# Scores a pair ahead, sampled keys by halves and the key tail's order, in the attention of a hybrid decoder step

## The chip, the core and the metric

The kernel runs on one core of a Trainium2 chip. It is one program that computes a whole inference step. The metric is the device time of one execution in microseconds (us). PE is TensorE, DVE is VectorE, ACT is ScalarE, POOL is GpSimd and SP is SyncE. Every one of them runs its own list of instructions in order, and they wait for each other only by semaphores.

## The reference, cut to what matters

Two layers, each on 256 prompt positions and on 8 sampled sequences of 4 new tokens with 2048 past positions each. Every layer has one input projection, an S5 state-space group, a sparse attention group with 8 query heads and 2 key/value heads, an output projection and a SwiGLU FFN. The change touches attention only. For each query head it is

```
def dense_gqa(q, k, v, dist, valid):
    s = einsum('...tkgd,...skd->...kgts', q, k) * HEAD_DIM ** -0.5
    s = s - alibi_slopes()[:, :, None, None] * dist[..., None, None, :, :]
    p = masked_softmax(s, valid[..., None, None, :, :])
    return einsum('...kgts,...skd->...tkgd', p, v), p
```

done three times (compressed blocks, the 16 of 33 key blocks of 64 with the highest summed compressed probability, and a sliding window of 512) and added with sigmoid gates. For the prompt every branch sees at most 256 keys. For the samples the selected branch has 2048 cached keys per sequence, which are read from a paged cache: 16 pages of 128 positions each, keys and values apart, 128 KB a page and kind.

## The kernel before

All activations lie in SBUF with the features on the partitions; 288 columns are the 256 prompt tokens and the 32 sampled ones. A layer is a hardware loop over the same code: projection with the state-space scan beside it, the compression of 256 cache pages by convolution, then **the attention middle** (at 683 to 797 us and 2556 to 2669 us in the profile), **the value stage** in which the cached values are weighted (to 882 and 2753 us), then output projection and FFN, which are plain streams of weights through PE.

In the attention middle two things run interleaved, by an order that is written out by hand in each engine's program.

- *Sampled keys.* The keys of the 8 sequences come in half groups: 2 halves (`hf`) of 4 groups (`g4`), each in two sets `e` (even and odd sequences). SP and POOL each load one half of every set, four pages, in `key_pages` (L286 to L297): four register loads of page numbers, then a wait for `kring_free`, then four DMAs. A set's buffer is free when `keys` (L820, on PE, matmuls at L827) has multiplied the set two before it. Two window sets of `keys` go first, then 16 cache sets, four for each pair of prompt heads. The scores of the 128 sampled rows land in banks 2 and 3 of PSUM (`PS[1]`, one bank for each key head, 512 columns). DVE adds the position bias and takes them to SBUF (`biased`, L1572), for a full group at once, and allows the next group with `kgroup_evac`.
- *Prompt heads.* The 8 heads go in pairs, `HEADS[0]` and `HEADS[1]`, each with two banks for scores (`h.s1`, `h.s0`; banks 0, 1 and 4, 5) and its own buffers. For a head: POOL copies its queries (`h.q`, L522) and gives `q_copied`; PE computes `scores` (L850, L856); DVE `prompt_bias` (L1640) adds the bias and takes maxima; ACT takes exponentials (L1200); DVE `prompt_scale` (L1656) normalizes (last operation at L1669); PE turns the probabilities (`turn_p`, L862, into banks 6 and 7); ACT takes them back (L1204 to L1206, `pt_evac`); PE weights the values (`weigh`, L873) into `h.s1`, the head's own score bank; DVE `prompt_out` (L1671) copies them out and gives `po_evac`, which the next `scores` of this buffer waits for.

The order on PE for a pair (`pair`, L884) is: scores of both heads, two `keys` sets, turn head a, one `keys` set, weigh a, turn b, one `keys` set, weigh b. On DVE: bias a, bias b, scale a, scale b, out a, the group of sampled keys, out b, then for the sampled keys the block mask (added at L1696) and the maxima (L1698). On POOL (L518 to L526), for pair i: the two query copies of pair i, then its four sets. So the copies for pair i+1 stand behind the last set of pair i.

After the fourth pair DVE takes the last maxima (`sw_max`), ACT takes the exponentials of the sampled scores (`SS`, 2080 wide, then `SW`, 544 wide, for both key heads, L1213), DVE normalizes (`sw_ready`), PE turns them in 12 steps through 6 banks (L922) and ACT takes each to `PTS` (L1222, L1226). Then the value stage: `values` (L311 to L322) loads 16 pages of each sequence from three queues ("full" by SP, "more" by POOL, "rest" by ACT, five or six pages each, again with register loads first), into two buffers in turn. The first needs all key sets done (`kring_free` 22); the second lies over `SS` and needs all 12 turns done (`st_done` 12).

Of the kernel before, what the change touches and what calls it, by code (L numbers as in the profile page):

```python
# [23 lines left out]
P = 128  # L24
# [84 lines left out]
def build(nc, T):  # L109
# [174 lines left out]
    with nc.Fori(0, L) as lay:  # L284
        with nc.Block() as block:
# [302 lines left out]
            QKG = [C_QN] * 4 + [C_KS, C_KW]  # L588

            @block.tensor  # L590
            def _(pe):
# [228 lines left out]
                def keys(hf, e, count, more=None):  # L820

                    pe.wait_ge(S[f"kset{e}_full"], count)
                    if more is not None:
                        pe.wait_ge(S[f"kset{e}_more"], more)
                    for k in range(NKV):
                        for j in range(4):
                            mm = pe.matmul(PS[1][32 * j:32 * j + 32, k, 256 * hf:256 * hf + 256].rearrange("p (g s) -> p g s", g=2),  # L827
                                           QPD[:, k, 2 * j + e, :], KR[4 * e + j][:, :, k, :], start=e == 0, stop=e == 1,
                                           tile_position=(0, 32 * j))
                    mm.then_inc(S["kring_free"], 1)  # L830

                pe.wait_ge(S["kgroup_evac"], 1)
# [51 lines left out]
                def pair(n, g4, k, peeled=False):  # L884
                    a, b_ = HEADS
# [17 lines left out]
                pair(0, 0, 0, peeled=True)  # L903
                pair(2, 1, 0)
                with pe.Fori(0, 2) as i:
                    pair(2 * i + GQA, i + 2, 1)
# [3 lines left out]
                pe.wait_ge(S["sw_ready"], 2)  # L910
                blocks = [(SS, x, P) for x in range(16)] + [(SS, 16, SMP)] + [(SW, x, P) for x in range(4)] \
                    + [(SW, 4, SMP)] + [(SCM, 0, NCMP)]
                for n in range(12):
                    if n >= 6:
                        pe.wait_ge(S["st_evac"], n - 5)
                    for m, (src, x, w) in enumerate(blocks[2 * n:2 * n + 2]):
                        if src is SW and x == 0:
                            pe.wait_ge(S["sw_ready"], 3)
# [1000 lines left out]
```

## Time and profile before

| | |
|---|---|
| median of 3 runs (lowest, highest) | 3755.5 us (3750.58, 3756.93) |
| the profiled execution, its own time | 3758.73 us |
| its span in the profile | 3757.2 us |
| PE busy | 3313.9 us, 88% |
| DVE / ACT / POOL busy | 48% / 32% / 21% |
| granted PE clock, mean | 0.924 |
| SP page issues of keys, POOL page issues of keys | 128 and 128, 128 KB each |
| median time from issue to landing of these | 2.4 us (SP), 2.9 us (POOL) |

The busy shares are means over stages with different limits. The change touches some 115 us of each layer, in which PE is not busy all the time, so what it is worth has to be read from the timelines of this stretch. Register loads and waits are not counted as busy; on POOL they show as idle time before a DMA ("issue").

### The profile page before, as it was taken

The numbers are of one execution on the slowest core, as the hardware profiler recorded it, in microseconds if no ns is written. First come the engines' busy times: TensorE is split into PE (matmuls) and PEld (weight loads), VectorE is DVE, ScalarE is ACT, GpSimd is POOL, SyncE is SP. The second block draws the span as 40 slices with busy tenths as digits, with TensorE's granted clock in tenths as the row PEclk, the third lists the DMA queues.
The fourth block names the chain that finished last, engine by engine and source line by source line (L and its number), as shares of the span: only waits on it lengthen the run. The fifth ranks groups of instructions, "written<-read, shape, count | busy, mean of one in ns | idle before, by whom it ended". The sixth has DMA issues, their size and how long they took to land. (4 is left out here: it accounts for less than half of the span.)

```text
span 3757.2 us, 62333 instructions
## 1 busy us (share of the span) xinstructions
PE 3313.9 (88%) x21882; PEld 2936.5 (78%) x21882; DVE 1820.4 (48%) x2671; ACT 1206.8 (32%) x1445; POOL 793.9 (21%) x1515
## 2 busy tenths in 40 slices
PE   6799699767899999999977995997678999999998
PEld 4566477546799999999955664775477999999998
DVE  4666555542433333444456665556433333334444
ACT  2011255232333333333320112552323333333333
POOL 1666523222100000000026664222221000000000
PEclk8788799878999999999977887998789999999999
DMA  4224535565344444444331244355653444444443
GB/s 156 77 98 167 190 108 186 169 210 194 134 151 162 158 172 161 156 164 171 113 121 68 93 191 163 126 177 172 217 193 117 157 170 165 156 172 163 157 159 134
DMA packets 142918, 579.44 MB, mean 154 GB/s; under 512 B 20817, under 2 KB 92658, under 8 KB 116530
## 3 DMA queue, kind: packets, MB, share of 16 engines
q1 hardware_dynamic: 106706, 491.88, 36.1%
q0 software_dynamic: 23968, 71.07, 5.8%
q10 hardware_dynamic: 12096, 14.69, 1.2%
q8 instruction: 72, 1.18, 0.1%
q14 instruction: 76, 0.62, 0.0%
HBM read 570.02 MB, written 24.18 MB: 158 GB/s over the span
## 5 line engine op out<-in xcount | busy, mean ns | idle before, releaser
L988 PE MATMUL banks<-normed_hi,weights_hi 128*128 128x288 f32 x4736 | 1408.1, 297 | 55.3 <-POOL normed_lo L534 34.1
L988 PE MATMUL banks<-normed_lo,weights_hi 128*128 128x288 f32 x4736 | 1399.8, 296 | 0.0
L988 PE MATMUL banks<-normed_hi,weights_lo 128*128 128x288 f32 x4736 | 1395.0, 295 | 0.0
L1327 DVE TENSOR_TENSOR weights_lo<-weight_slots,weights_hi 128x2048 fp32r<-128x2048 f32 x296 | 680.7, 2300 | 1103.5 <-ACTq L1252 1103.5
L988 PEld LDWEIGHTS banks<-normed_hi,weights_hi 128*128 128x128 f32 x4736 | 890.3, 188 | 57.9 <-issue 55.0
L1249 ACT ACTIVATE weights_hi<-weight_slots 128x2048 fp32r<-128x2048 f32 x296 | 567.0, 1916 | 1142.6 <-PE banks L988 1134.8
L988 PEld LDWEIGHTS banks<-normed_hi,weights_lo 128*128 128x128 f32 x4736 | 894.7, 189 | 0.0
L988 PEld LDWEIGHTS banks<-normed_lo,weights_hi 128*128 128x128 f32 x4736 | 892.1, 188 | 0.6
L344 DVE TENSOR_TENSOR arena<-arena 128x192 f32<-128x192 f32 (+5 forms) x800 | 425.4, 553 | 44.8
L344 POOL TENSOR_TENSOR arena<-arena 128x64 f32<-128x64 f32 (+5 forms) x800 | 408.0, 520 | 86.2 <-issue 0.7
L605 PE MATMUL banks<-normed,weight_slots 128*128 128x288 f32 x1664 | 421.9, 417 | 0.0
L605 PEld LDWEIGHTS banks<-normed,weight_slots 128*128 128x128 f32 x1664 | 324.9, 196 | 97.3 <-issue 6.0
L794 PE MATMUL banks<-conv_high,conv_weights 128*128 128x508 f32 x1024 | 335.4, 409 | 27.1 <-DVE conv_low_a L1327 18.8
L794 PEld LDWEIGHTS banks<-conv_high,conv_weights 128*128 128x128 f32 x1024 | 194.8, 192 | 82.2 <-issue 15.4
L1175 ACT ACTIVATE conv_high<-arena 128x512 fp32r<-128x512 f32 x256 | 158.0, 628 | 172.7 <-PE banks L794 172.5
L308 POOL DMA_DIRECT2D arena<-in_cache_cmp x256 | 137.4, 537 | 317.0 <-issue 303.5
L483 POOL DMA_DIRECT2D params<-in_params x2 | 1.2, 616 | 865.2 <-issue 865.2
L1037 ACT ACTIVATE projected<-banks 128x576 f32 (+1 forms) x28 | 18.2, 651 | 419.6 <-PE banks L605 401.5
L657 PE MATMUL banks<-arena 128*32 128x288 f32 x256 | 32.7, 685 | 129.4 <-issue 129.4
L657 PEld LDWEIGHTS banks<-arena 128*32 128x32 f32 x256 | 13.4, 161 | 144.6 <-issue 144.6
L1327 DVE TENSOR_TENSOR conv_low_a<-arena,conv_high 128x512 fp32r<-128x512 f32 x128 | 86.6, 691 | 79.1 <-ACT conv_high L1175 77.7
L1327 DVE TENSOR_TENSOR conv_low_b<-arena,conv_high 128x512 fp32r<-128x512 f32 x128 | 87.7, 691 | 69.9 <-ACT conv_high L1175 68.8
(271 smaller groups left out, 2683.0 us busy)
## 6 DMA issues: line engine op xcount, KB each, us to landing
weight_slots<-in_w_gu SPq DMA_DIRECT2D x88, 2048.0 KB, 7.6
weight_slots<-in_w_down SPq DMA_DIRECT2D x44, 2048.0 KB, 7.7
weight_slots<-in_w_in SPq DMA_DIRECT2D x28, 2048.0 KB, 7.7
arena<-in_cache_cmp SPq DMA_DIRECT2D x256, 128.0 KB, 3.3
arena<-in_cache_cmp POOLq DMA_DIRECT2D x256, 128.0 KB, 3.4
weight_slots<-in_w_out SPq DMA_DIRECT2D x16, 2048.0 KB, 7.9
arena<-in_cache_slc_k SPq DMA_DIRECT2D x128, 128.0 KB, 2.4
arena<-in_cache_slc_k POOLq DMA_DIRECT2D x128, 128.0 KB, 2.9
```

The costliest lines, as they stand in the source:

```text
L308: eng.dma_start(AR[:, o:o + 256], T["cache_cmp"][bass.ds((lay * 160 + page) * 2 + k, 1)] .rearrange("a p x -> p (a x)")).then_inc(S[f"raw{ ...
L344: return eng.tensor_tensor(out, a, b, op)
L483: pool.dma_start(PR[:, :], row("params", lay)).then_inc(S["params_in"], 16)
L605: mm = pe.matmul(banks_[:, m, 0:TOK], WR[:, s, c, 128 * m:128 * m + 128], rhs(first + c), start=start and c == 0, stop=stop and c == k - 1)
L657: mm = pe.matmul(PS[2][o:o + 32, j // 4, 0:TOK], CBS[:, j, r, :], HS[:, j, r, :], start=r == 0, stop=r == 1, tile_position=(0, o))
L794: mm = pe.matmul(acc, w, x, start=i == hf == 0 and x is hi and w is wh, stop=i == 15 and hf == 1 and x is lo)
L988: mm = pe.matmul(out, wt[:, hf, col], x[:, rhs + c, :], start=begin and c == 0 and i == 0, stop=hf == 1 and c == k - 1 and i == 2, skip_gr ...
L1037: act.activation(dst, src, ACT.Copy).then_inc(S[sem], by)
L1175: act.activation(HRG[:, n % 4, :].rearrange("p (g x) -> p g x", x=16), RAW[u % 2][:, :, i, :], ACT.Copy)\
L1249: w = act.activation(WH[:, hf, :], WR[:, s, 8 * hf:8 * hf + 8, :].rearrange("p a b -> p (a b)"), ACT.Copy)
L1327: return dve.tensor_tensor(out, a, b, op)
```

## The change

It rewrites the order of the attention middle; what is computed stays the same.

- PE: `scores` of pair i+1 move from behind both `weigh` of pair i to before `turn_p` of pair i. Scores no longer wait for `po_evac` but for `ps_max`. Both `weigh` now stand at the end of the pair, write to bank 3 and wait for `po_evac` once a pair. All eight `keys` halves write 256 columns for each key head into bank 2, and the first set of each half waits for `kgroup_evac` of the half before it, the window halves too.
- DVE: sampled keys go out by halves (256 columns, `keys_out`); the bias of the next pair stands between the two halves; both heads' outputs go out in one copy behind the second half.
- ACT: the exponentials of pair i+1 stand behind the `pt_evac` of pair i.
- The pair loops are written out, with constant addresses.
- Tail: `SW` before `SS` in exponentials, normalization and turns (`TURNS`), and ACT's five value pages of the first sequence (`values(act, 0, 0, "rest")`) move from before the exponentials to behind them.
- The programs of POOL and SP are not changed.

```diff
+            TURNS = [9, 10, 11] + list(range(9))
@@ PE
-                def keys(hf, e, count, more=None):
+                def keys(n, e, count, more=None):
...
+                    if e == 0:
+                        pe.wait_ge(S["kgroup_evac"], n + 1)
...
-                            mm = pe.matmul(PS[1][32 * j:32 * j + 32, k, 256 * hf:256 * hf + 256].rearrange("p (g s) -> p g s", g=2),
+                            mm = pe.matmul(bank(2)[32 * j:32 * j + 32, 256 * k:256 * k + 256].rearrange("p (g s) -> p g s", g=2),
...
-                pe.wait_ge(S["kgroup_evac"], 1)
...
                 def scores(n, h, k):
                     pe.wait_ge(S["q_copied"], n + 1)
-                    pe.wait_ge(S["po_evac"], n + 1)
+                    if n >= 2:
+                        pe.wait_ge(S["ps_max"], n - 1)
...
                 def weigh(n, h, k):
                     pe.wait_ge(S["pt_evac"], n + 2)
-                    o = h.s1
+                    if n % 2 == 0:
+                        pe.wait_ge(S["po_evac"], n + 2)
+                    o = bank(3)[:, 256 * (n % 2):256 * (n % 2) + 256]
...
+                scores(0, a, 0)
+                scores(1, b_, 0)
+                for i in range(4):
+                    n = 2 * i
                     def part(hf, e):
-                        keys(hf, e, g4 * 128 + 64 * hf + 192, g4 * 128 + 64 * hf + 64)
-                    scores(n, a, k)
-                    scores(n + 1, b_, k)
-                    pe.wait_ge(S["kgroup_evac"], g4 + 2)
+                        keys(2 + n + hf, e, 128 * i + 64 * hf + 192, 128 * i + 64 * hf + 64)
                     part(0, 0)
                     part(0, 1)
-                    if peeled:
+                    if i == 0:
                         mask()
+                    if i < 3:
+                        scores(n + 2, a, (n + 2) // GQA)
+                        scores(n + 3, b_, (n + 3) // GQA)
                     turn_p(n, a)
                     part(1, 0)
-                    weigh(n, a, k)
+                    part(1, 1)
                     turn_p(n + 1, b_)
-                    part(1, 1)
-                    weigh(n + 1, b_, k)
+                    weigh(n, a, n // GQA)
+                    weigh(n + 1, b_, n // GQA)
...
+                for i, n in enumerate(TURNS):
+                    if i >= 6:
+                        pe.wait_ge(S["st_evac"], i - 5)
+                    if i in (0, 3):
+                        pe.wait_ge(S["sw_ready"], 2 if i == 0 else 3)
@@ ACT
+                for j, h in enumerate(HEADS):
+                    prompt_exp(j, h)
+                for i in range(NQ // 2):
                     for j, h in enumerate(HEADS):
                         act.wait_ge(S["pt_done"], 2 * i + j + 3)
...
-                values(act, 0, 0, "rest")
+                    if i < 3:
+                        for j, h in enumerate(HEADS):
+                            prompt_exp(2 * i + 2 + j, h)
 
                 act.wait_ge(S["sw_max"], 1)
-                for i, v in enumerate((SS, SW)):
+                for i, v in ((1, SW), (0, SS)):
...
+                values(act, 0, 0, "rest")
@@ DVE
-                dve.wait_ge(S["kring_free"], 6)
-                for k in range(NKV):
-                    biased(SW[:, k, 0:WIN], dw[:, 0:WIN], k, PS[1][:, k, :])
-                dve.drain().then_inc(S["kgroup_evac"], 1)
+                for hf in range(2):
+                    dve.wait_ge(S["kring_free"], 2 * hf + 4)
+                    for k in range(NKV):
+                        biased(SW[:, k, 256 * hf:256 * hf + 256], dw[:, 256 * hf:256 * hf + 256], k, bank(2)[:, 256 * k:256 * k + 256])
+                    dve.drain().then_inc(S["kgroup_evac"], 1)
...
+                for i in range(NQ // 2):
                     n = 2 * i
                     prompt_scale(n, a)
                     prompt_scale(n + 1, b_)
-                    prompt_out(n, a)
...
+                    keys_out(i, 0)
+                    if i < 3:
+                        prompt_bias(n + 2, a)
+                        prompt_bias(n + 3, b_)
+                    keys_out(i, 1)
+                    prompt_out(n)
```

## Rows read from the trace of the kernel before

**Rows 1.** windows: length, PE, PEld, DVE, ACT, POOL busy, PE clock, DMA share, GB/s

```profile
725.13:746.04 20.91, 15.62 (x125) 10.35 (x124) 13.50 (x38) 7.11 (x30) 9.32 (x18) 0.92 0.67 199
...
814.00:882.00 68.00, 43.24 (x776) 32.39 (x776) 11.39 (x26) 8.80 (x19) 16.66 (x32) 0.80 0.87 294
```

**Rows 2.** timeline of POOL, layer 0: start, us, operation, count [idle before, releaser]

```profile
697.34 2.31 POOL L294 DMA_DIRECT2D arena<-in_cache_slc_k  x4 [12.93 <-PE banks L827]
702.30 2.32 POOL L294 DMA_DIRECT2D arena<-in_cache_slc_k  x4 [2.66 <-issue]
...
714.64 0.74 POOL L522 COPY squares<-projected 128x256 f32 x2
719.24 0.54 POOL L294 DMA_DIRECT2D arena<-in_cache_slc_k  x1 [3.85 <-PE banks L827]
721.81 1.73 POOL L294 DMA_DIRECT2D arena<-in_cache_slc_k  x3 [2.04 <-issue]
...
778.82 2.32 POOL L294 DMA_DIRECT2D arena<-in_cache_slc_k  x4 [2.66 <-issue]
```

**Rows 3.** timeline of POOL, layer 1, same columns

```profile
2569.73 2.31 POOL L294 DMA_DIRECT2D arena<-in_cache_slc_k  x4 [12.65 <-PE banks L827]
...
2632.35 1.26 POOL L522 COPY squares<-projected 128x256 f32 x2
...
2652.58 2.32 POOL L294 DMA_DIRECT2D arena<-in_cache_slc_k  x4 [2.64 <-issue]
```

**Rows 4.** timeline of TensorE, layer 0, same columns

```profile
694.70 1.93 PE L827 MATMUL banks<-arena 128*32 128x256 f32 x16 [4.34 <-DMA arena<-in_win_k]
...
714.71 0.47 PE L866 MATMUL banks<-consts,weight_slots 128*128 128x128 f32 x1 [3.78 <-DVEq L1669]
...
716.61 1.94 PE L827 MATMUL banks<-arena 128*32 128x256 f32 x16
...
720.68 0.33 PE L866 MATMUL banks<-consts,weight_slots 128*128 128x128 f32 x1
...
721.70 1.07 PE L827 MATMUL banks<-arena 128*32 128x256 f32 x16
723.00 0.70 PE L877 MATMUL banks<-weight_slots,v_rows 128*128 128x256 f32 x2 [0.22 <-ACTq L1207]
...
725.13 0.71 PE L856 MATMUL banks<-projected,squares 128*128 128x128 f32 x4
...
728.74 1.07 PE L827 MATMUL banks<-arena 128*32 128x256 f32 x16
...
788.84 1.07 PE L827 MATMUL banks<-arena 128*32 128x256 f32 x16 [2.25 <-DMA arena<-in_cache_slc_k]
789.84 0.78 PE L877 MATMUL banks<-weight_slots,v_rows 128*128 128x256 f32 x2
```

**Rows 5.** timeline of TensorE, layer 1, same columns

```profile
2572.55 1.22 PE L856 MATMUL banks<-projected,squares 128*128 128x128 f32 x4
...
2577.59 1.07 PE L827 MATMUL banks<-arena 128*32 128x256 f32 x16
```

**Rows 6.** timeline of VectorE, layer 0, same columns

```profile
691.83 2.49 DVE L1327 TENSOR_TENSOR arena<-arena 64x1089 f32<-64x1089 f32 x2
...
793.98 1.28 DVE L1327 TENSOR_TENSOR arena<-arena  x2
```

**Rows 7.** timeline of ScalarE, layer 0, same columns

```profile
791.15 2.42 ACTq L320 DMA_DIRECT2D arena<-in_cache_slc_v  x5
797.30 2.03 ACT L1213 ACTIVATE arena<-arena,smalls 128x2080 f32<-128x2080 f32 x1 [9.56 <-DVE smalls L1708]
...
805.01 0.60 ACT L1222 ACTIVATE arena<-banks 128x512 f32<-128x512 f32 x1 [1.48 <-PE banks L922]
...
813.53 0.39 ACT L1222 ACTIVATE arena<-banks 127x256 f32<-127x256 f32 x1
816.90 2.77 ACTq L320 DMA_DIRECT2D arena<-in_cache_slc_v  x5
```

More of the change, by code:

```diff
@@ L1194, in _, with prompt_exp @@
                 act.drain().then_inc(S["c_exp"], 1)
-                with act.Fori(0, NQ // 2) as i:
-                    for j, h in enumerate(HEADS):
-                        act.wait_ge(S["ps_max"], 2 * i + j + 1)
-                        for c, v in enumerate([h.p1[:, 0], h.p1[:, 1], h.p0[:, 0], h.p0[:, 1], h.pc[:, 0], h.pc[:, 1]]):
-                            act.activation(v, v, ACT.Exp, bias=h.m[:, c:c + 1], accum_out=h.d[:, c:c + 1])
-                        act.drain().then_inc(S["p_exp"], 1)
+                def prompt_exp(n, h):
+                    act.wait_ge(S["ps_max"], n + 1)
+                    for c, v in enumerate([h.p1[:, 0], h.p1[:, 1], h.p0[:, 0], h.p0[:, 1], h.pc[:, 0], h.pc[:, 1]]):
+                        act.activation(v, v, ACT.Exp, bias=h.m[:, c:c + 1], accum_out=h.d[:, c:c + 1])
+                    act.drain().then_inc(S["p_exp"], 1)
+                for j, h in enumerate(HEADS):
+                    prompt_exp(j, h)
+                for i in range(NQ // 2):
                     for j, h in enumerate(HEADS):
@@ L1215, in _ @@
                         act.drain().then_inc(S["sw_exp"], 1)
+                values(act, 0, 0, "rest")
                 widths = [P] * 16 + [SMP] + [P] * 4 + [SMP] + [NCMP]
-                for n in range(12):
-                    act.wait_ge(S["st_done"], n + 1)
+                for i, n in enumerate(TURNS):
+                    act.wait_ge(S["st_done"], i + 1)
                     w = widths[2 * n:2 * n + 2]
-                    src = bank([0, 1, 4, 5, 6, 7][n % 6])
+                    src = bank([0, 1, 4, 5, 6, 7][i % 6])
                     if len(set(w)) == 1:
@@ new lines, in keys_out @@
+                def keys_out(i, hf):
+                    c = slice(512 * i + 256 * hf, 512 * i + 256 * hf + 256)
+                    dve.wait_ge(S["kring_free"], 4 * i + 2 * hf + 8)
+                    for k in range(NKV):
+                        biased(SS[:, k, c], ds_[:, c], k, bank(2)[:, 256 * k:256 * k + 256])
+                    dve.drain().then_inc(S["kgroup_evac"], 1)
+                a, b_ = HEADS
+                prompt_bias(0, a)
+                prompt_bias(1, b_)
+                dve.wait_ge(S["mask_done"], 1)
@@ L1691, in pair @@
-                    dve.drain().then_inc(S["kgroup_evac"], 1)
-                    prompt_out(n + 1, b_)
-                    for k in range(NKV):
-                        v = SS[:, k, bass.ds(i * 512, 512)].rearrange("p (j s) -> p j s", s=SEL)
-                        tt(v, v, MB[:, k, bass.ds(i * 8, 8)].unsqueeze(2).to_broadcast([P, 8, SEL]), ALU.add)
+                    keys_out(i, 0)
+                    if i < 3:
+                        prompt_bias(n + 2, a)
+                        prompt_bias(n + 3, b_)
@@ L1700, in _ @@
-                dve.wait_ge(S["tables_back"], 16)
-                pair(0, peeled=True)
-                with dve.Fori(1, 4) as i:
-                    pair(i)
+                        dve.tensor_reduce(mxs[:, k, i:i + 1], SS[:, k, 512 * i:512 * i + 512], AXX, ALU.max)
                 dve.drain()
```

47 lines of the change are left out of this document (15 added, 32 removed).

## The prediction, written before the changed kernel ran

> **What bounds the kernel now.** I read the page first (PE 88% busy), then the windows of the attention middle, then the timeline of each engine there. In a window of one pair of heads PE works 15.6 of 20.9 us and the DMA share is 0.67, against 0.87 in the value stage [rows 1]: neither the array nor the transfers bound this stage. Two loops run through it side by side. The first is the chain of a pair, scores, bias, exponential, scale, turn, weigh, out: PE sits idle 3.78 us before the first turn and waits there for DVE [rows 4]. The change is aimed at this one. The second is POOL's list. A set of four pages takes 2.32 us of issues and 2.66 us of register loads before them, and the two query copies of a pair 0.74 us [rows 2]. Four sets and the copies make 4 x (2.32 + 2.66) + 0.74 = 20.7 us, and the pair's window has 20.9. So POOL already sets the pace, and shortening the first loop alone could take at most what POOL waits: its sets run from 697.34 to 781.14 (83.8 us) in layer 0 and from 2569.73 to 2654.90 (85.2 us) in layer 1 [rows 2, 3], against 16 x 2.32 + 15 x 2.66 + 3 x 0.74 = 79.2 us.
>
> **The sum is made against the profiled execution,** 3758.7 us, 3.2 above the median of 3755.5 us; the difference is put on the median at the end.
>
> **Scores ahead: a new loop through POOL.** Scores of heads n+2 and n+3 now stand on PE before the turn of head n and before the third set of keys. They need the query copies, and POOL makes these behind the pair's fourth set. That fourth set needs the second `keys` of the same pair, so POOL can't have it early. What is queued behind the waiting scores: both turns, two `keys` sets, both weighs. Who waits for that: POOL's and SP's first set of the next pair, which needs the third `keys`. So a round can't be shorter than this chain:
>
> - four sets with three groups of register loads: 4 x 2.32 + 3 x 2.66 = 17.3 us [rows 2]; the fourth group of loads is hidden in the wait;
> - the first query copy and its signal: half of 0.74 us and 0.1, 0.5 us [rows 2];
> - scores of two heads: 3.61 us at the upper clock level (725.13 to 728.74) [rows 4], 5.04 us where they began at the lower level (2572.55 to 2577.59) [rows 5]. PE will have waited for the copy by then, as it had in the 3.78 us before 714.71, where a turn then took 1.90 us instead of 1.02 (714.71 to 716.61, 720.68 to 721.70) [rows 4]. I take 5.0;
> - the turn, 1.02 us, and `keys`, 1.07 us, with the level back up (1.90 and 1.94 at the lower one) [rows 4];
> - from the end of `keys` to POOL's first issue: 696.63 to 697.34, 0.7 us [rows 2, 4].
>
> Sum 25.6 us a round. Bounds: 17.3 + 0.5 + 3.6 + 1.0 + 1.1 + 0.3 = 23.8 us, if the array keeps the upper level and the signal is short, and 17.3 + 0.9 + 6.7 + 1.9 + 1.9 + 0.8 = 29.5 us with all of it at the lower level (the scores' 3.61 us stretched as the turn is, 1.90 to 1.02). There are three such rounds in a layer, and one of them keeps the 2.04 us stall inside POOL's first set of the second pair [rows 2]. The last pair has no scores behind it, and its four sets take their 17.3 us. All sets then take 3 x 25.6 + 2.0 + 17.3 = 96.1 us: 12.3 us more than now in layer 0, 10.9 us in layer 1. The bounds give 90.7 and 107.8 us, so 5.5 to 24.0.
>
> The other effects of this part cost nothing while POOL is that late. The `ps_max` wait, the halves' `kgroup_evac` waits and the bias between the halves all lie in the 8 us in which POOL issues its last set. The written-out loops save a few issue gaps there.
>
> **The window halves.** PE's first `keys` of the second half ran at 694.70 [rows 4]. It now needs DVE's first half to be out, and DVE is in the comparisons until 694.32 [rows 6]; two additions of 256 columns (an estimate of 0.4 us each: 2.49 us for 2 x 1089 columns is 0.3 for 256, and something fixed) and a signal give 695.3. POOL's first set starts 0.6 us later; bounds 0 and 1.
>
> **The last sets' tail.** The last page set arrives as late behind its issue as now (781.14 to 788.84 [rows 2, 4]). Now `keys`, one weigh and one copy follow, and DVE begins the mask at 793.98, 5.1 us after 788.84 [rows 4, 6]. After the change `keys`, the turn of head 7, two weighs and a double copy stand between, as DVE takes the outputs before the mask. PE will have stood idle for some 8 us, so at the lower level: 1.9 + 1.9, then a weigh of 2.9 (2.1 us at the upper level from 723.00 to 725.13, 3.6 where the level fell from 789.84 on [rows 4]), a second of 2.1, the copy 0.7 (ACT's of 512 columns takes 0.60 [rows 7]): 9.6 us with signals. That is 4.5 us more; bounds 2 and 6.
>
> **The ScalarE handover.** ACT's five pages of the first sequence went out at 791.15, while ACT waited for the maxima [rows 7]: their price was nothing. They now stand behind the four exponentials and before the 12 copies of turned scores. A call of `values` on ACT costs its register loads too: after the last copy (813.92) the next call's issues began at 816.90 and ended at 819.67, 5.8 us [rows 7]. From the start of the exponentials at 797.30 they end 6.2 us later (805.01 less the 1.48 idle), the call takes 5.8, and the 12 copies 8.2 (805.01 to 813.92, less the short waits for PE): 20.2 us against 16.6. The windows' turns going first gain nothing, because ACT is in `SS`'s exponentials and the call by then. So 3.6 us later at the end and some 2.5 to 3 at the twelfth turn, which starts the second buffer's load. I take 3.2; bounds 0 (value stage absorbs it) and 3.7. What follows is a double-buffered stream of loads at a DMA share of 0.87 [rows 1], which makes nothing up.
>
> **Sum.** Layer 0: 12.3 + 0.6 + 4.5 + 3.2 = 20.6. Layer 1: 10.9 + 0.6 + 4.5 + 3.2 = 19.2. Together +39.8 us: 3798.5 against the profiled run, 3795 against the median.
>
> **Two rules weighed.** The query copies are on the path now. Their usual 0.74 us became 1.26 us at 2632.35 [rows 3]. The Trainium skill ("SBUF — State Buffer", Who interferes with whom) says that a DVE instruction with two SBUF inputs blocks a GpSimd one that reads SBUF. By it the copies stay short, since DVE will be idle and waiting for these very scores; by the stretched row each round gains 0.3 to 0.5 us, 3 us in all.
>
> The same skill ("TensorE: Matmul & The Clock Gate", HAM oscillation — how this bites in real kernels) says that an array that waits on data in every round restarts at its lower clock in every round. The turn's 1.90 us after a wait agrees. Without the rule the scores would cost 3.6 us instead of 5.0, 8 us less in all, and the result would be 3787.
>
> **Rivals.**
> *A, faster:* the first loop decides and POOL's copies come in time. For it speaks PE's idle 3.78 us before a turn. Against it, the copies stand behind the fourth set, and a pair already fills POOL. It decides if PE reaches the scores after the copies, which needs a round of PE's own work above 25 us where it has 15.6. POOL's waits of 4.6 and 6.0 us would go, 1.2 come back at the window halves: some 9 us less, 3746.
> *B, no change:* POOL's later sets only fill slack before the value stage. The sets' end and the mask are linked in one chain (788.84 to 793.98), so there is no slack. 3755.
> *C, slower by half:* rounds at 23.8 us and the handover absorbed: 2 x (6.2 + 0.6 + 2) = 18 us, 3773. For it: DVE and SP are not slowed.
> *D, slower still:* all of the loop at the lower level, 29.5 us: 2 x (23.3 + 0.6 + 6 + 3.7) = 67 us, 3822. For it: PE will idle in each round. Against it: the level was back 4 us after a wait, at 720.68 [rows 4].
>
> **How the numbers follow.** Mine 0.68, C 0.15, D 0.09, A 0.04, B 0.04. The predicted time is 3795. The range leaves out A, B and the far half of C and D: 3774 to 3811. A measurement of this kernel tells 0.2% (7.5 us) from no change: faster 0.04, within it 0.04, slower 0.92.
>
> **What would show it.** POOL's first set of pair i+1 should start 25 to 26 us after that of pair i, and its idle time before it be released by PE's L827. PE should be idle some 4 to 8 us before each later `scores`, released by POOL, and hardly before a turn. The mask should begin 9 to 10 us after the last `keys` starts, and five ACT issues should lie between the last exponential and the first copy of turned scores. I am wrong if POOL's rounds stay at 21 us, or if the value stage begins late but ends at its old distance from the last key set.

## The result, and the profile after

| | before | after |
|---|---|---|
| median of 4 runs beside each other (lowest, highest) | 3756.22 us (3750.58, 3757.8) | 3805.68 us (3802.0, 3811.0) |
| profiled execution, its span | 3757.2 us | 3802.3 us |
| granted PE clock, mean | 0.924 | 0.915 |

The changed kernel is slower: ratio 1.0131 (95% interval 1.0118 to 1.0143), 49.5 us on the medians and 45.1 us between the two profiled spans. The prediction said 3795 us and 39.8 us.

First the windows of the changed kernel, one round of POOL and the value stage, in the columns of [rows 1]:

```profile
755.03:781.42 26.39, 16.95 (x128) 11.97 (x124) 13.45 (x40) 7.11 (x30) 9.32 (x19) 0.74 0.50 160
836.00:904.00 68.00, 43.06 (x737) 32.23 (x739) 11.00 (x25) 12.19 (x26) 18.77 (x35) 0.77 0.84 280
```

The 26.39 us are POOL's third round, from its first set to that of the next pair; it is 5.5 us longer than the 20.91 of before, while DVE, ACT and POOL are busy for the same time. PE is busy 1.3 us more at a lower granted clock (0.74 for 0.92), and the transfers' share fell from 0.67 to 0.50. So the time is waiting, and not work.

The timeline of POOL shows where, in layer 0 (columns as in [rows 2]):

```profile
701.56 2.31 POOL L294 DMA_DIRECT2D arena<-in_cache_slc_k  x4 [14.05 <-PE banks L830]
...
718.86 1.20 POOL L522 COPY squares<-projected 128x256 f32 x2
727.43 0.54 POOL L294 DMA_DIRECT2D arena<-in_cache_slc_k  x1 [7.37 <-PE banks L830]
730.01 1.73 POOL L294 DMA_DIRECT2D arena<-in_cache_slc_k  x3 [2.04 <-issue]
...
746.72 0.74 POOL L522 COPY squares<-projected 128x256 f32 x2
755.03 2.32 POOL L294 DMA_DIRECT2D arena<-in_cache_slc_k  x4 [7.57 <-PE banks L830]
...
772.27 0.74 POOL L522 COPY squares<-projected 128x256 f32 x2
781.42 2.32 POOL L294 DMA_DIRECT2D arena<-in_cache_slc_k  x4 [8.40 <-PE banks L830]
...
796.37 2.32 POOL L294 DMA_DIRECT2D arena<-in_cache_slc_k  x4 [2.67 <-issue]
```

After each pair's copies POOL waits for PE's `keys` (now L830) 7.4 to 8.4 us, of which some 2.7 are its own register loads. The rounds are 25.9, 27.6 and 26.4 us, and all sets take 97.1 us (701.56 to 798.69) where they took 83.8. And PE, in the same stretch (columns as in [rows 4]), waits for those copies:

```profile
719.31 1.22 PE L859 MATMUL banks<-projected,squares 128*128 128x128 f32 x4 [5.09 <-POOL squares L522]
...
724.66 0.31 PE L869 MATMUL banks<-consts,weight_slots 128*128 128x128 f32 x1
...
725.66 1.93 PE L830 MATMUL banks<-arena 128*32 128x256 f32 x32
...
747.17 1.22 PE L859 MATMUL banks<-projected,squares 128*128 128x128 f32 x4 [5.97 <-POOL squares L522]
...
772.73 1.22 PE L859 MATMUL banks<-projected,squares 128*128 128x128 f32 x4 [5.72 <-POOL squares L522]
...
778.65 0.31 PE L869 MATMUL banks<-consts,weight_slots 128*128 128x128 f32 x1
```

Scores from their first matmul to the turn behind them took 5.35 us (719.31 to 724.66) and 5.92 us (772.73 to 778.65), against 3.61 us at the full clock in [rows 4]. The windows of the round between them, cut where the level changes, show why:

```profile
747.17:750.50 3.33, 3.33 (x12) 2.97 (x13) 0.00 (x0) 0.00 (x0) 0.29 (x1) 0.52 0.16 53
750.50:752.26 1.76, 1.76 (x15) 1.66 (x14) 0.00 (x0) 0.00 (x0) 0.00 (x0) 1.00 0.00 0
```

PE had been idle for 5.97 us; its clock was granted at 0.52 (nearly all at the level of 1.2 GHz) for the first 3.3 us of scores, and at 1.00 (2.4 GHz) behind that. In the rounds before and after it the first 3.5 us of scores had 0.50.

The end of the middle, first PE, then DVE, then ACT, in layer 0:

```profile
807.74 1.94 PE L830 MATMUL banks<-arena 128*32 128x256 f32 x16 [10.43 <-DMA arena<-in_cache_slc_k]
...
815.14 0.69 PE L886 MATMUL banks<-weight_slots,ssm_out 15*128 15x256 f32 x2
```

```profile
697.87 0.87 DVE L1581 SCALAR_TENSOR_TENSOR arena<-consts,banks 128x256 f32<-128x256 f32 x2 [0.44 <-issue]
...
815.94 0.69 DVE L1683 COPY normed<-banks 128x512 f32<-128x512 f32 x1 [5.33 <-PE banks L886]
816.55 1.28 DVE L1336 TENSOR_TENSOR arena<-arena 128x512 f32<-128x512 f32 x2
```

```profile
819.78 0.75 ACT L1221 ACTIVATE arena<-arena,smalls 128x544 f32<-128x544 f32 x1 [7.05 <-DVE smalls L1719]
...
829.27 2.44 ACTq L320 DMA_DIRECT2D arena<-in_cache_slc_v  x5
831.75 0.60 ACT L1231 ACTIVATE arena<-banks 128x512 f32<-128x512 f32 x1 [5.75 <-PE banks L925]
```

The mask starts 8.8 us behind the last `keys` (807.74 to 816.55; before, 788.84 to 793.98, 5.1 us). ACT's first copy of turned scores starts 12.0 us behind its first exponential (819.78 to 831.75; before, 797.30 to 805.01, 7.7 us), with register loads and the five issues in between.

Between anchors that both kernels have (the load of the tie table ahead of the stretch, POOL's first and last set, the last `keys`, the mask, the first exponential, the first matmul of the output projection) the two profiles give, in us, layer 0 / layer 1:

| stretch | before | after | more | forecast |
|---|---|---|---|---|
| tie table to first set | 14.2 / 13.9 | 15.3 / 15.5 | 1.1 / 1.5 | 0.6 |
| first to last set | 83.8 / 85.2 | 97.1 / 97.4 | 13.3 / 12.3 | 12.3 / 10.9 |
| last issue to last `keys` | 7.7 / 7.6 | 9.05 / 8.6 | 1.35 / 1.0 | 0 |
| last `keys` to mask | 5.1 / 3.7 | 8.8 / 8.6 | 3.7 / 4.9 | 4.5 |
| mask to first exponential | 3.3 / 3.3 | 3.2 / 3.2 | -0.1 | 0 |
| first exponential to output projection | 98.2 / 97.2 | 100.1 / 99.9 | 1.9 / 2.7 | 3.2 |
| together | 212.3 / 210.9 | 233.7 / 233.2 | 21.3 / 22.3 | 20.6 / 19.2 |

That is 43.6 of the 45.1 us between the profiled spans.

### The profile page after: what moved, and what is told of

It reads as the page before. It is cut to its first block, busy times and chain, and to the rows that moved or that the text cites. A ratio compares the mean times of both kernels' runs of the same rounds, so it can differ in the third digit from the quotient of the medians.

```text
span 3802.3 us, 62159 instructions
## 1 busy us (share of the span) xinstructions
PE 3323.5 (87%) x21882; PEld 2947.9 (78%) x21882; DVE 1819.2 (48%) x2683; ACT 1206.8 (32%) x1445; POOL 795.0 (21%) x1515
## 4 chain that ended last, share of the span: by engine, by line
PE 36%; DVE 5%; issue 3%; DVEq 1%; ACT 1%; DMA 1%; POOLq 1%; ACTq 1%; SPq 1%; POOL 0%; PEld 0%; PEldq 0%
PE banks L991 25%; PE banks L795 4%; DVE arena L344 3%; PE banks L606 3%; PE banks L645 1%; DVEq L358 1%; POOLq L289 1%; PE banks L658 0%; PE banks L859 0%; ACTq L315 0%; ACTq L320 0%; DMA arena<-in_cache_slc_v 0%; DVE arena L1336 0%; DVEq L383 0%; PE banks L598 0%
## 5 line engine op out<-in xcount | busy, mean ns | idle before, releaser
L606 PEld LDWEIGHTS banks<-normed,weight_slots 128*128 128x128 f32 x1664 | 325.2, 196 | 97.4 <-issue 6.0
L795 PEld LDWEIGHTS banks<-conv_high,conv_weights 128*128 128x128 f32 x1024 | 194.4, 192 | 82.2 <-issue 15.3
```

The source lines that it names most:

```text
L606: mm = pe.matmul(banks_[:, m, 0:TOK], WR[:, s, c, 128 * m:128 * m + 128], rhs(first + c), start=start and c == 0, stop=stop and c == k - 1)
L795: mm = pe.matmul(acc, w, x, start=i == hf == 0 and x is hi and w is wh, stop=i == 15 and hf == 1 and x is lo)
```

## The experiments

Each was timed beside the kernel before on the same chip; the ratio is to that kernel, with its 95% interval. The kernel before itself read 3756.1 to 3757.4 us in these batches. Differences to the changed kernel are taken from its 3805.7 us, which stands on a batch of its own with the kernel before at 3756.2 us. Each kernel has one profile, so a row of a single profile can be off by what varies from kernel to kernel; where that matters it is said.

### The copies alone

In the changed kernel only POOL's program is edited: the query copies of pair i+1 stand between the two halves of pair i. The same edit serves in five later kernels.

```diff
-                with pool.Fori(0, NQ // 2) as i:
-                    q_copies(i)
+                q_copies(0)
+                with pool.Fori(0, NQ // 2 - 1) as i:
                     for hf in range(2):
+                        if hf:
+                            q_copies(i + 1)
                         for e in range(2):
                             key_pages(pool, i, hf, e, "more")
+                for hf in range(2):
+                    for e in range(2):
+                        key_pages(pool, 3, hf, e, "more")
```

> The changed kernel with one edit: POOL copies the queries of the next pair between its second and third page set instead of behind the fourth. Theory (the new loop through POOL's copies sets the rounds): the rounds fall from 25.5 to 29 us to 21 to 22 us, POOL's sets of a layer from 97 to 80 to 84 us, PE waits for POOL before no scores any more, and the time falls by 26 to 32 us, from 3806 to some 3777. Rival (half groups in one bank, with DVE's evacuation between them, lengthen the rounds whatever the copies do): rounds stay at 24 us or more and the time falls by less than 12 us. Rival (only the clock level after the waits): rounds fall by no more than 2 us each, 12 us in all.

Measured: 3766.2 us (3760.0 to 3768.7), ratio 1.0027 (1.0017 to 1.0036), 39.5 us less than the changed kernel. POOL's timeline:

```profile
698.12 2.31 POOL L294 DMA_DIRECT2D arena<-in_cache_slc_k  x4 [14.32 <-PE banks L838]
...
705.39 0.74 POOL L522 COPY squares<-projected 128x256 f32 x2
708.53 2.31 POOL L294 DMA_DIRECT2D arena<-in_cache_slc_k  x4 [2.39 <-issue]
...
719.64 0.54 POOL L294 DMA_DIRECT2D arena<-in_cache_slc_k  x1 [3.84 <-PE banks L838]
```

The waits of 7 to 8 us are gone, the rounds are 21.5, 22.7 and 20.4 us, and all sets take 80.7 and 80.9 us: 16.4 and 16.5 less. In this profile no `scores` waits for POOL any more. So the place of the copies behind the fourth set is what carries the 13 us a layer of the result. The gain of 39.5 us is above the 26 to 32 us that were expected; the sets alone give 32.9.

Two smaller things lie in it. There are 2.39 us behind the copy, where sets without a copy between them have 2.65, as in [rows 2]. And the edit also writes the last pair's sets out of the loop, with constant indices:

```profile
762.78 2.32 POOL L294 DMA_DIRECT2D arena<-in_cache_slc_k  x4 [2.72 <-issue]
767.36 2.32 POOL L294 DMA_DIRECT2D arena<-in_cache_slc_k  x4 [2.26 <-issue]
```

There the idle time between sets is 2.26 us, and the last pair's four sets take 16.1 us where they took 17.3 in the changed kernel. So 1.2 us a layer of the gain are this, and not the copies' place.

### Three single edits around the end

ACT's five pages go back to before the exponentials, in the changed kernel:

```diff
+                values(act, 0, 0, "rest")
                 act.wait_ge(S["sw_max"], 1)
                 ...
-                values(act, 0, 0, "rest")
```

> The changed kernel with ScalarE's five value pages of the first sequence put back before the wait for the maxima. Theory (the handover costs 3.2 us a layer): the first copy of turned scores starts 6 to 7 us after the first exponential instead of 12, the last ends some 16.5 us after it instead of 20.1, and the time falls by 6 to 8 us, to 3799. Rival (the value stage starts earlier but is bound by its loads and absorbs it): the copies end earlier but the time stays within 2 us of 3806.

Measured: 3795.1 us, ratio 1.0108 (1.0091 to 1.0125), 10.6 us less than the changed kernel. First exponential to first copy is 6.3 us instead of 12.0 and the copies take 9.9 to 10.1 us instead of 8.2. The gain is above the 6.4 us that the prediction priced for both layers. The trace doesn't give all of it to the pages: the first exponential to the output projection is only 2.7 and 1.5 us shorter than in the changed kernel, while the last `keys` start 7.1 and 4.2 us behind POOL's last issue instead of 9.05 and 8.6. Why they come sooner here was not tested.

The mask of the last group goes before the outputs of heads 6 and 7, in the changed kernel:

```diff
                     keys_out(i, 1)
-                    prompt_out(n)
+                    if i < 3:
+                        prompt_out(n)
 ...
                 dve.drain().then_inc(S["sw_ready"], 1)
+                prompt_out(6)
```

> The changed kernel with VectorE's copy of the last two heads' outputs put behind the last block mask and maxima. Theory (the mask waits for two weighs): the mask starts 2 to 3 us after the last keys instead of 8.7 us, and the time falls by 12 to 13 us, to 3793. Rival (the wait is only for the array at its lower clock level, or the exponentials are held by something else): the mask starts earlier but the exponentials do not, and less than 4 us is won.

Measured: 3793.45 us, ratio 1.0104 (1.0087 to 1.0120), 12.2 us less. DVE, layer 0, from the last bias to the mask:

```profile
807.05 0.88 DVE L1581 SCALAR_TENSOR_TENSOR arena<-consts,banks 128x256 f32<-128x256 f32 x2 [9.89 <-PE banks L830]
808.04 1.29 DVE L1336 TENSOR_TENSOR arena<-arena 128x512 f32<-128x512 f32 x2
```

The mask starts 1.0 us behind the start of the bias and 3.0 us behind the last `keys`, where it was 8.8. So the turn, two weighs and the double copy stood in front of it, as the tail step said. (In this profile too the last `keys` come sooner behind the last issue, 4.5 and 6.8 us.)

The pages' move by itself, on the kernel before (same lines as above, the other way round):

> The kernel before with only the move of ScalarE's five value pages behind the exponentials. Theory: the five issues and their register loads cost 3 to 4 us a layer between the last exponential and the first copy of turned scores, so 6 to 8 us in all, 3763. Rival (absorbed by the value stage): within 2 us of 3756.

Measured: 3763.96 us (3759.9 to 3769.3), ratio 1.0022 (1.0012 to 1.0032), 7.8 us more than before on the medians. ACT, layer 0:

```profile
800.96 2.03 ACT L1212 ACTIVATE arena<-arena,smalls 128x2080 f32<-128x2080 f32 x1 [9.63 <-DVE smalls L1708]
...
810.47 2.42 ACTq L320 DMA_DIRECT2D arena<-in_cache_slc_v  x5
812.93 5.49 ACT L1222 ACTIVATE arena<-banks 128x512 f32<-128x512 f32 x8 [5.74 <-PE banks L922]
```

The exponential starts when it started before, relative to the mask, and the first copy 12.0 us behind it. The handover costs about what the prediction gave it, and without anything else of the change: 3.9 us a layer by the medians, and 3.1 and 2.6 us by the stretch from the first exponential to the output projection (101.3 and 99.8 us). In this kernel the tie table to the first set is 15.3 and 15.0 us, though nothing of that stretch was edited: it was the one profile of the kernel before that was short there (14.2 and 13.9), so the 1.1 to 1.6 us in the first row of the table of stretches are not shown to be the window halves' doing.

### The three edits together

Copies, pages and mask, all in the changed kernel:

> The changed kernel with all three edits so far: POOL's copies between its second and third set, ScalarE's five pages before the maxima, the last outputs' copy behind the last mask. Theory (three separate costs on one path, so they add): 39.5 + 10.6 + 12.2 us less than 3805.7, 3743, some 12 us under the kernel before; POOL's sets take 80 to 81 us a layer and nothing but its own list holds it. Rival (with POOL's wait gone the pair's own chain or VectorE becomes the bound, and the gains overlap): above 3750.

Measured: 3759.5 us (3753.8 to 3765.0), ratio 1.0002 (0.9992 to 1.0012): a miss of 16 us. From the kernel with the copies alone the two other edits take only 6.7 us off, where each took 10.6 and 12.2 off the changed kernel. Mask to first exponential is 7.75 and 7.6 us here, and 3.2 to 3.3 in every kernel so far. ACT shows the reason:

```profile
788.79 0.60 ACT L1218 ACTIVATE weight_slots<-banks 128x512 f32<-128x512 f32 x1 [12.62 <-PE banks L881]
...
793.18 2.44 ACTq L320 DMA_DIRECT2D arena<-in_cache_slc_v  x5
795.66 0.75 ACT L1230 ACTIVATE arena<-arena,smalls 128x544 f32<-128x544 f32 x1 [5.75 <-issue]
```

DVE had the maxima at 791.1, but ACT's list held head 7's turned weights (788.79), then 3.3 us of register loads and 2.44 us of issues. The call had cost nothing before the exponentials only because the mask was late. The two edits paid for the same stretch. This late start is 4.4 us a layer, some 9 of the 16 us. The rest isn't placed by an experiment; what the traces show is that the two single edits' profiles had last `keys` that came 1.8 to 4.6 us sooner behind the last issue than in the changed kernel, while here they take 7.5 and 8.0 us, about as with the copies alone (7.6 and 6.8).

### Filled waits

In the changed kernel eight matmuls of constants, whose output the scores overwrite, stand before the scores of each coming pair, behind a wait for the maxima that free their bank:

```diff
                     if i < 3:
+                        pe.wait_ge(S["ps_max"], n + 1)
+                        for _ in range(8):
+                            pe.matmul(a.s1[:, 0:256], ident, CT[:, 0:256], start=True, stop=True)
                         scores(n + 2, a, (n + 2) // GQA)
```

> The changed kernel with eight extra matmuls (128x256, result unused) on PE before each later pair of scores, in the time in which it waits for POOL's copies. Theory (the wait lets the array fall to its lower clock level, and the scores behind it cost 5.1 to 5.9 us instead of 3.6): with the level kept, the scores take 3.6 to 4.2 us, a round is 1 to 2 us shorter, and the time falls by 6 to 12 us, to 3797. Rival (the level does not follow this filling, or the scores are bound by something else): within 3 us of 3806, or slower where the extra work outlasts the wait.

Measured: 3791.8 us (3789.9 to 3796.3), ratio 1.0085 (1.0069 to 1.0102), 13.9 us less than the changed kernel with 48 more matmuls. PE, then the windows of the same scores:

```profile
741.60 4.21 PE L904 MATMUL banks<-consts 128*128 128x256 f32 x16
747.72 0.71 PE L859 MATMUL banks<-projected,squares 128*128 128x128 f32 x4 [1.90 <-POOL squares L522]
...
751.25 0.31 PE L869 MATMUL banks<-consts,weight_slots 128*128 128x128 f32 x1
```

```profile
747.72:749.50 1.78, 1.78 (x13) 1.68 (x13) 0.00 (x0) 0.00 (x0) 0.29 (x1) 1.00 0.28 101
...
```

The scores take 3.53 us at a clock of 1.00, where they took 5.09 with 3.3 of them at 0.52. In the five other rounds of the two layers they take 3.4 to 3.5 us as well. The rounds are 24.2, 26.0 and 24.0 us and all sets 91.5 us. So of the 12 to 13 us by which the sets became longer, 5.6 and 5.9 are the clock level after PE's wait, and the rest is the order of POOL's list itself. The forecast of 6 to 12 us was a little low. Between the two profiles the sets are 11.5 us shorter in both layers together, and the whole stretch of the table 10.4; the medians differ by 13.9, and the trace doesn't place the rest.

### The landing of the last pages

On the kernel before, SP issues `w_out`'s 2 MB behind the wait for the last keys, not ahead of it:

```diff
-                slot_load(J_OUT, slot(0), row("w_out", lay * 8))
                 sp.wait_ge(S["kring_free"], 22)
+                slot_load(J_OUT, slot(0), row("w_out", lay * 8))
```

> The kernel before with one edit: SyncE issues the first 2 MB load of the output weights behind its wait for the last key set's use instead of right behind its own last issue. The last page set lands 7.6 to 7.7 us behind POOL's last issue before, against a median of 2.9. Theory (it shares the 16 DMA engines with those 2 MB, issued 0.7 us before POOL's last issue ends): it lands in 2.5 to 4.5 us, 3 to 5 us less a layer, so 3746 to 3750. Rival (the landing is long for another reason, or the 2 MB delay the value pages as much): within 2 us of 3756.

Measured: 3749.9 us (3746.5 to 3754.0), ratio 0.9980 (0.9970 to 0.9990): faster than the kernel before, by 7.4 us. The last issue to the last `keys` is 5.4 us in both layers instead of 7.7. The transfers around the last set of layer 0, first in the kernel before the change (776 to 790 us), then in the changed one (794 to 808 us); the columns are KB each and the median us from issue to landing:

```profile
weight_slots<-in_w_out SPq DMA_DIRECT2D x1, 2048.0 KB, 10.1
arena<-in_cache_slc_k POOLq DMA_DIRECT2D x5, 128.0 KB, 3.3
arena<-in_cache_slc_k SPq DMA_DIRECT2D x4, 128.0 KB, 2.6
```

```profile
weight_slots<-in_w_out SPq DMA_DIRECT2D x1, 2048.0 KB, 11.1
arena<-in_cache_slc_k SPq DMA_DIRECT2D x4, 128.0 KB, 2.4
arena<-in_cache_slc_k POOLq DMA_DIRECT2D x4, 128.0 KB, 5.1
```

POOL's pages of the last set run beside the 2 MB. With the load behind them the last landing is 2.3 us a layer shorter, so the long landing is partly the 2 MB beside it. These are 4.5 of the 7.4 us. The first exponential to the output projection is shorter too, 94.1 and 95.0 us instead of 98.2 and 97.2, which was not looked into. The landing is 1.0 to 1.35 us longer in the changed kernel, with POOL's pages at 5.1 us, though the load is at the same place behind SP's last set. It is not shown that the change does this: with the load in place the last `keys` start 6.6 to 7.8 us behind the last issue in the three kernels with the order of before, and 4.2 to 9.2 us in the six with the changed order. In layer 1 it is 4.2 us in the kernel with ACT's pages moved and 8.6 in the changed kernel, though those pages go out only behind the last `keys`.

### Everything mended

Copies, pages, mask and the late `w_out` in the changed kernel, and there too the first window half on DVE before the two comparisons:

```diff
+                win_out(0)
                 tt(sel[0], other, own, ALU.is_gt)
                 tt(sel[1], other, own, ALU.is_equal)
                 dve.drain()
-                for hf in range(2):
-                    ...
+                win_out(1)
```

> The three edits of the run before the last two, with the late load of the output weights and with VectorE taking out the first window half before its comparisons. Theory: 3743 less 8 us of the landing and 1 to 2 us of the window half, 3734. Rival (the landing is not the output weights' doing): 3741 to 3744.

Measured: 3750.2 us (3743.3 to 3756.6), ratio 0.9980 (0.9970 to 0.9990), 9.3 us less than with three edits. Against 3734 this is a miss of 16 us, and it is the same 16: the expectation started from 3743, which the three edits hadn't reached, and the 9 to 10 us more that it forecast came. The landing is 3.35 and 2.7 us, and ACT's call is again in the way: mask to first exponential 7.8 and 7.6 us. The first window half early gains nothing: the tie table to the first set takes 14.4 and 15.4 us, but from the tie table to the end of the last issue it is 96.7 and 96.9 us, and it was 96.6 and 96.4 with three edits.

Then the same with ACT's call moved ahead of its copies of head 7:

```diff
                     for j, h in enumerate(HEADS):
+                        if i == 3 and j == 1:
+                            values(act, 0, 0, "rest")
                         act.wait_ge(S["pt_done"], 2 * i + j + 3)
```

> The kernel with all parts mended, and in it one more edit: ScalarE's five value pages of the first buffer stand before its copy of head 7's turned weights instead of before the exponentials. In the mended kernel the trace shows ScalarE ready with head 7 at 787.6, then 3.3 us of register loads and 2.44 us of issues, and the first exponential at 793.4, though the maxima were there at 788.8. My theory: the register loads now fall into the 8.7 us in which ScalarE waits for head 7's turn, the issues end near 787.0, the copy of head 7 is 0.5 us late, and the first exponential starts 3.2 us behind the mask's start instead of 7.7: 4.4 us less a layer, 3741 to 3744. Rival 1: the value pages' landing sets the start of the value stage, so an earlier exponential gives nothing: 3748 to 3751. Rival 2: the issues, asked for while the last keys' pages and POOL's value pages are under way, lengthen head 7's weigh and give half back: 3745 to 3747.

Measured: 3745.9 us (3743.7 to 3747.1), ratio 0.9971 (0.9960 to 0.9983). It has the lowest median of all. ACT, then DVE, layer 0:

```profile
787.04 2.50 ACTq L320 DMA_DIRECT2D arena<-in_cache_slc_v  x5
789.59 0.60 ACT L1219 ACTIVATE weight_slots<-banks 128x512 f32<-128x512 f32 x1 [9.07 <-issue]
...
791.06 0.75 ACT L1230 ACTIVATE arena<-arena,smalls 128x544 f32<-128x544 f32 x1 [0.35 <-DVE smalls L1731]
```

```profile
793.09 0.69 DVE L1694 COPY normed<-banks 128x512 f32<-128x512 f32 x1 [1.68 <-PE banks L893]
```

The exponential starts 3.2 us behind the mask again, 4.4 us earlier, as expected. But the issues ended at 789.5 and not 787.0, so head 7's copy came late, its weigh too, and DVE's double copy at 793.09 holds up the normalization of `SW`. The twelve copies end some 1.2 us later behind the first exponential. About half of the expected gain arrived (3.4 us by the ratios, 4.4 by the medians), near what rival 2 said.

### Two controls on the kernel before

The copies between the halves, nothing else:

> Control on the kernel before: only POOL's query copies move, to between the two halves of the pair before, as in the kernel with only the copies moved. My theory (copies matter only where scores are asked for a pair ahead): POOL's list keeps its 20.7 us a pair wherever the copies stand in it, so the sets stay at 83 to 85 us from first to last and the time at the kernel before's, within 4 us of 3757. Rival (an earlier copy is worth something by itself, since PE's scores wait 1 to 2 us for it in each pair): 2 to 3 us less a layer, sets in 81 us as in the other kernels with moved copies, 3751. Then up to 6 of the 39.5 us that the same edit took off the changed kernel were never part of the change's cost.

Measured: 3751.8 us (3748.4 to 3758.5), ratio 0.9986 (0.9977 to 0.9995), 4.9 us less. The rival had the number, but its reason fails: in the kernel before PE never waits for a copy. The copies of 714.64 [rows 2] are done 9.7 us ahead of the scores at 725.13 [rows 4], and the next two pairs' copies 6.8 and 8.3 us ahead of theirs. The row of 725.13 shows no idle time before it, and neither does that of any other `scores` of the three later pairs in either layer. The sets don't carry the gain clearly either: they take 82.7 and 83.3 us, and in the three kernels with the copies at their old place 83.8 and 85.2, 83.6 and 83.3, 83.7 and 82.9. What can be read is that the last pair's sets, written out by the same edit, stand 4.6 us apart instead of 5.0, and that the last `keys` start 6.6 us behind the last issue instead of 7.6 to 7.8. Why this kernel is 5 us faster stays open. Still, up to 5 of the 39.5 us that the edit took off the changed kernel are to be had without the change. With the copies moved in both, the change's other parts cost some 15 us (1.0027 against 0.9986), so the 49.5 us are 39.5 that the edit gives back, 15 for the rest, less 5 that the same edit takes off the kernel before.

And the copies with the late `w_out`:

> The kernel before with two edits that need none of the change: SP issues w_out's load behind the wait for the last keys, and POOL's query copies stand between the two halves of the pair before. Alone they gave 0.9980 and 0.9986 of the time before, -7.4 and -4.9 us. What it tells apart is whether the change's own order (scores ahead, half groups, windows first) is worth anything once its three costs are mended. If the two edits add up, 3744 to 3747, the same as the 3745.9 of the changed kernel with everything mended, and the order is worth nothing. Rival: the order shortens the last keys' tail by about 1 us a layer (the mask 3.0 us behind the last keys instead of 3.7 to 4.0) and the copies' gain is swallowed by the late w_out: 3748 to 3751, and the order is worth 2 to 5 us.

Measured: 3750.9 us (3746.0 to 3754.9), ratio 0.9986 (0.9977 to 0.9995). The two edits don't add up: the sets take 83.5 and 82.8 us and the landing is 5.8 and 6.7 us. By the medians the mended changed kernel is 5 us better, by the ratios' intervals (0.9960 to 0.9983 against 0.9977 to 0.9995) the two overlap a little. The time lies in the rival's 3748 to 3751. The stretch from tie table to output projection is 204.2 and 204.6 us in the mended changed kernel and 207.5 and 208.8 in this one, of which the landing is 3.1 and 3.8. But the two profiled spans (3744.3 and 3745.1 us) differ by only 0.8 us, so the 7.4 us of the stretch are not in them. So whether the change's own order is worth something once it is mended stays open; if it is, it is a few us.

## Why the prediction was right

The size was off by 5 us of 45 in the profiles (10 of 49.5 on the medians), and the mechanism held: the loop through POOL's copies was forecast at 23.2 of the 39.8 us and measured at 25.6 of 45.1. That the sum came so near is partly luck, because errors had both signs: the sets, the landing and the stretch before the first set were forecast 6 us too low in the two layers together, the handover 1.8 us too high. Step by step:

- **Rounds through POOL, right, slightly low.** Forecast 25.6 us a round, with one that keeps the stall. Measured 25.9, 27.6, 26.4 in layer 0, and in layer 1 the timeline reads:

```profile
2593.12 2.31 POOL L294 DMA_DIRECT2D arena<-in_cache_slc_k  x4 [14.19 <-PE banks L830]
...
2618.69 0.54 POOL L294 DMA_DIRECT2D arena<-in_cache_slc_k  x1 [7.56 <-PE banks L830]
...
2647.76 2.31 POOL L294 DMA_DIRECT2D arena<-in_cache_slc_k  x4 [9.12 <-PE banks L830]
...
2673.30 2.31 POOL L294 DMA_DIRECT2D arena<-in_cache_slc_k  x4 [7.56 <-PE banks L830]
```

  25.6, 29.1 and 25.5 us. The mis-sized terms are layer 1's round with the stall, 29.1 where 27.6 was forecast, and the scores after the wait, 5.1 to 5.9 us where I took 5.0. Rival A fell with this: PE waited 5.1 to 6.3 us for the copies before all six later pairs of scores. So did C and D: rounds at neither 23.8 nor 29.5 us (the 29.1 hold the stall of 2.0).
- **The clock, right.** The lower level after PE's wait gave the scores 5.1 to 5.9 us, and filled waits gave back 13.9 us. The 8 us that the prediction set apart as what the clock adds were too small. By the rule of the Trainium skill ("TensorE: Matmul & The Clock Gate", HAM oscillation — how this bites in real kernels), which the prediction weighed, an array that waits on data every round restarts at its lower clock every round; the trace agrees, with 0.50 to 0.52 in the first 3.3 to 3.5 us of the scores in each of layer 0's three rounds. One reading of the prediction was loose: 720.68 is 6.0 us behind the turn at 714.71, and not 4.
- **The copies' length, small.** They took 1.20 us in layer 0's first round, where DVE was not idle but still in its normalization (a multiplication of three parts that takes 1.13 us elsewhere took 1.53 beside them), and 0.74 us in the later rounds, where DVE was idle. In layer 1's first round they took 0.74 beside DVE's work, and it was DVE's instructions that took longer (0.52 and 1.23 us instead of 0.30 and 1.13). By the rule of the Trainium skill ("SBUF — State Buffer", Who interferes with whom) a DVE instruction with two SBUF inputs contends with a GpSimd one that reads SBUF; the trace agrees, with 1.20 us for the copies in the one first round and the longer DVE instructions in both. What the prediction took from it, that the copies stay short because DVE waits, holds for the later rounds.
- **Window halves, not told apart.** 0.6 us forecast. The first half comes out at 697.87, 0.4 us behind the comparisons, in 0.87 us for both heads as assumed. But the stretch varies between 13.9 and 15.9 us over kernels with and without the halves.
- **Landing unchanged, wrong by 1.0 to 1.35 us a layer.** The step took 7.7 us over from before. It measured 9.05 and 8.6; the load of `w_out` beside it is a part of what it is, as the late load showed. Whether the change lengthens it is not shown.
- **Tail, right.** 4.5 us forecast, 3.7 and 4.9 measured. As a length it was forecast at 9.6 us and took 8.8 and 8.6; layer 1's comes out above 4.5 because the kernel before took only 3.7 us there, where the sum used layer 0's 5.1 for both. Its price by itself is 6 us a layer by the experiment, because the order without it is better than that of the kernel before (3.0 us to the mask instead of 5.1 and 3.7).
- **ScalarE handover, right in kind, a little high.** 3.2 us a layer forecast, 1.9 and 2.7 measured. By itself on the kernel before it cost 3.9 us a layer by the medians, 3.1 and 2.6 in the traces. First exponential to first copy is 12.0 and 11.8 us, as computed.
- **B fell:** the sets took 12 to 13 us longer and the output projection came 21 to 22 us later behind the tie table.

What the prediction didn't see, and didn't need, is that the kernel before had something to gain from the same edit, 5 us. It isn't the same weakness: no `scores` waited for a copy there.

## What to carry to other kernels

Before work is put a stage ahead on one engine, follow every signal that it needs to the list of the engine that gives it: if that engine gives it behind work which itself waits for this stage, the two lists now meet once a round, and the round becomes the sum of both halves. Here moving the producer's two instructions in its list gave back 39.5 us, and the reorder that needed them was worth a few us at most. A call that is free in front of a late event is free because of that event: when the event is made earlier, look at what stands in front of it, for two edits that each pay for the same stretch don't add up. And where PE's wait can't be taken away, work without a use in it can pay for itself, here 13.9 us for 48 matmuls.

## What the runs showed of the hardware

In the round shown, PE worked on constants for 4.2 us (eight matmuls, 16 records), was idle for 1.9 us and then ran the scores at 1.00 from their first matmul (747.72). Without that work, after 5.97 us of idle time, they had 0.52 for their first 3.3 us. In the last round of both layers the added work was slower, 5.3 and 5.8 us, and no idle time is left between it and the scores.

Register loads ahead of DMAs are dear on the two engines whose gaps were read: 2.65 us for four on POOL in the loop, 2.26 us where the last pair is written out with constant indices, and 3.3 us for ACT's call of five pages. Behind a copy the gap on POOL was some 0.3 us shorter (2.39 instead of 2.65), so little of them runs beside it.

With a 2 MB load in flight POOL's 128 KB pages had a median of 3.3 us (before) and 5.1 us (changed kernel) to landing, and SP's, issued just ahead of the load, 2.6 and 2.4 us; over the whole run of the kernel before it is 2.9 and 2.4 us. With the load behind them the last `keys` came 2.3 us sooner behind their issue.
